# Another last instruction on GpSimd: a tensor_tensor on one column becomes an affine_select on a 128x128 mask

## The chip, the cores and the metric

The kernel runs on one core of one Trainium2 chip. The metric is the device time of one execution in microseconds (us), the median of three runs of the same program. One of the three is also recorded by the hardware profiler.

## What is computed

Three transformer layers in float32, on 256 tokens of width 1024:

```
x = first_block(x, ...)        # attention with causal mask and distance bias, then squared-ReLU MLP
return second_block(x, c, ...) # even_layer: gated convolution + RG-LRU, then SwiGLU
                               # odd_layer: stick-breaking attention, then SwiGLU
```

The first thing that happens to x is a norm and a projection, which is where this case plays:

```
def rms_norm(x, gain):
    y = xf * lax.rsqrt(jnp.mean(xf * xf, axis=-1, keepdims=True) + RMS_EPS)
u = rms_norm(h, norm_mix_pre[layer])
q, k, v = jnp.split(x @ w_qkv, 3, axis=-1)
```

The stick-breaking attention masks its scores strictly below the diagonal, `strict = k_pos < q_pos`. The two layers of the second block take shift, scale and gate vectors from `silu(c) @ ada_w + ada_b`.

## The kernel before

The program is written engine by engine: each engine has one in-order instruction stream, and semaphores tie them together. There is no scheduler. The 256 tokens are two tiles of 128 (t = 0, 1). All weights (about 205 MB) stream from HBM through four buffers `w_raw`. ScalarE (ACT) rounds each part to `w_hi` (line 747), VectorE (DVE) computes the remainder `w_lo` (line 1178), and TensorE (PE) multiplies hi by hi, hi by lo and lo by hi.

The **start**. GpSimd (POOL) makes the constants. It writes `ones` (line 665, semaphore `consts` becomes 1), clears `ident` (line 667), turns it into the identity with an affine_select (line 668), clears `rg_w` (line 670, `consts` becomes 2), fills `neg_dist` with iota (lines 673 and 675), builds `sb_mask` (lines 677 and 678), masks `neg_dist` (line 682), and then three times clears 2048 columns of `mod` and loads a bias row into them (lines 631 and 632). PE waits for `consts` 1, runs two warm-up matmuls (line 2236) and spreads the gain row over the partitions (line 2241). Then it waits for `consts` 2, since everything that follows begins with transposes of the normed x by the identity: `norm_T` (line 1940), four transposes for each half of a tile. ACT copies them out of PSUM to `aT` (line 811), and PE starts on the products of the first projection (line 2064). ACT's own order there is: squares and rstd of tile 0 (lines 769, 853 and 854), w_hi of weight parts 0 and 1 (line 747), aT (line 811), squares of tile 1.

The **middle**. POOL adds up the partitions of the partial sums of `ada_w` with partition_all_reduce (line 661), in groups spread over the program, and between the groups it does small tensor_scalar and tensor_tensor operations for the norms (lines 643 and 652 to 655) and some memsets.

The **end of POOL's program**. `partition_sums` for `GATE_F` (line 661, two instructions) and then one tensor_tensor on `var[:, 0:1]` (line 721), whose result nobody reads. POOL has nothing after that.

The built program has an extra POOL instruction at several places, which the source does not write: it is shown as `ISA` without operands and as MODIFY_POOL_CONFIG in the trace. One stands before the first affine_select (line 668), one before each group of partition_all_reduce (line 661), and one before the first tensor_scalar or tensor_tensor that follows such a group (lines 643, 652 and 721). In this text it is called the reload. The two kinds are told apart by what follows: into set A (iota, tensor_scalar, tensor_tensor) and into set B (partition_all_reduce). Memset and DMA have none anywhere.

Of the kernel before, what the change touches and what calls it, by code (L numbers as in the profile page):

```python
# [28 lines left out]
ALU = mybir.AluOpType  # L29
# [3 lines left out]
P = 128  # L33
# [10 lines left out]
NEG = -1e30  # L44
# [70 lines left out]
def block_program(nc, a, out):  # L115
    ctx = ExitStack()
    with ctx:
        def sb(name, shape, dt=F32):
            return ctx.enter_context(nc.sbuf_tensor(name, shape, dt))
# [28 lines left out]
        sb_mask = sb("sb_mask", [P, P])  # L148
# [5 lines left out]
        half_sums = sb("half_sums", [P, 4])  # L154
        var = sb("var", [P, 2])
# [260 lines left out]
        def parts_to(u, i=None, per=0):  # L416

            return plus(2 * u, i, 2 * per)
# [199 lines left out]
        def _(pool):  # L618
# [38 lines left out]
            def partition_sums(src, dst, done, count, step):  # L657

                for n in range(src.shape[-1] // CH):
                    pool.wait_ge(done, count + step * n)  # L660
                    pool.partition_all_reduce(dst[:, n * CH:(n + 1) * CH], src[:, n * CH:(n + 1) * CH], P,  # L661
                                              bass.bass_isa.ReduceOp.add).then_inc(pool_sum, 1)
# [6 lines left out]
                                       base=0, pattern=[[-1, P]], channel_multiplier=1))  # L669
# [9 lines left out]
                               pattern=[[-1, P]], channel_multiplier=1).then_inc(consts, 1)  # L679
            for lo, n, q0 in ((0, P, 0), (P, TOK, P)):  # L680
                part = neg_dist[:, lo:lo + n]
                pool.affine_select(out=part, in_=part, compare_op=ALU.is_ge, fill=NEG, base=q0,
                                   pattern=[[-1, n]], channel_multiplier=1).then_inc(consts, 1)
# [34 lines left out]
            rstd_halves()  # L718
            pool.wait_ge(xn_done, 24)
            partition_sums(GATE_F, GATE_F, w_used, parts_to(U_SG1 + 8), 6)  # L720
            pool.tensor_tensor(var[:, 0:1], half_sums[:, 1:2], half_sums[:, 0:1], ALU.add)


        @block.scalar
# [1794 lines left out]
```

## Time and profile before

| | us |
|---|---|
| median of 3 runs | 879.93 |
| lowest and highest | 879.71 and 880.51 |
| the profiled execution, its own time | 880.51 |
| its span in the trace | 878.7 |
| PE busy in the span | 869.1 (99%) |
| POOL busy in the span | 112.7 (13%) |

The span counts from the start of the recording to the last instruction's end; 1.81 us of the profiled execution's own time lie outside it. Busy time of PE includes waits inside its pipeline; what can be read safely is when its groups start. In a row of the timeline the two first numbers are start and duration in us, and the bracket behind it is the idle time of that engine before it with what ended it; "issue" means that it waited for nothing that the profile shows. PEld is the weight load of TensorE, and an engine's name with a q behind it is its sequencer.

### The profile page before, as it was taken

What the parts mean: (1) busy time and instruction counts of PE and PEld (TensorE: products, weight loads), DVE (VectorE), ACT (ScalarE), POOL (GpSimd) and SP (SyncE); (2) the same over time, 40 slices, a digit from 0 to 9 for tenths busy, and PEclk for the clock granted to TensorE, in tenths of its full rate; (3) what the DMA queues carried; (4) which work ended last, traced back from release to release, by engine and by line L of the source; (5) the groups of instructions that cost most, each with busy time, mean ns of one, the idle gap of its engine ahead of it and who ended that gap; (6) DMA issues with size and microseconds to landing.
All of it is one profiled execution on the core that took longest, in us unless ns stands there. A gap on an engine that the chain in (4) does not pass through costs nothing.

```text
span 878.7 us, 13239 instructions
## 1 busy us (share of the span) xinstructions
PE 869.1 (99%) x4806; PEld 739.7 (84%) x4806; DVE 714.6 (81%) x737; ACT 490.6 (56%) x663; POOL 112.7 (13%) x79
## 2 busy tenths in 40 slices
PE   8999999999999999999999999999999999999998
PEld 5998878888888799979888888878777888888887
DVE  6698987999898987898989899787897866655656
ACT  6545665565556657755555455555775365545542
POOL 5000100032110103026010411012000101100000
PEclk9999999999999999999999999999999999999999
DMA  7979567899889484547998798546434386666662
GB/s 243 346 248 355 173 211 296 319 366 358 322 324 339 159 287 146 176 160 216 386 329 309 269 353 302 180 137 216 135 113 142 96 245 190 190 192 190 191 192 72
DMA packets 117238, 208.07 MB, mean 237 GB/s; under 512 B 7252, under 2 KB 81340, under 8 KB 112072
## 3 DMA queue, kind: packets, MB, share of 16 engines
q1 hardware_dynamic: 116710, 205.31, 68.7%
q10 hardware_dynamic: 290, 2.10, 0.7%
q8 instruction: 28, 0.46, 0.2%
q14 instruction: 18, 0.15, 0.1%
q0 software_dynamic: 192, 0.05, 0.0%
HBM read 206.39 MB, written 1.05 MB: 236 GB/s over the span
## 4 chain that ended last, share of the span: by engine, by line
PE 93%; DVE 3%; DMA 2%; ACT 1%; issue 1%; POOL 0%; SPq 0%; DVEq 0%; POOLq 0%
PE ub L1968 11%; PE tp L1968 11%; PE acc L1826 7%; PE acc L1827 7%; PE acc L1829 7%; PE ub L1970 5%; PE tp L1970 5%; PE acc L1789 5%; PE acc L1790 5%; PE acc L1791 5%; PE acc L1954 3%; PE acc L1956 3%; PE acc L1955 3%; PE tp L2031 2%; PE acc L2064 1%; PE acc L1982 1%
## 5 line engine op out<-in xcount | busy, mean ns | idle before, releaser
L1178 DVE TENSOR_TENSOR w_lo<-w_raw,w_hi 128x1024 fp32r<-128x1024 f32 x271 | 343.3, 1283 | 78.1 <-ACT w_hi L747 77.6
L747 ACT ACTIVATE w_hi<-w_raw 128x1024 fp32r<-128x1024 f32 x271 | 283.9, 1056 | 202.7 <-PE acc L1829 41.5
L1968 PE MATMUL tp<-aT,w_hi 128*128 128x512 f32 x432 | 135.9, 396 | 0.0
L1968 PE MATMUL ub<-aT,w_hi 128*128 128x512 f32 x432 | 135.4, 395 | 0.0
L1826 PE MATMUL acc<-w_hi,hT_hi 128*128 128x512 f32 x266 | 103.9, 390 | 0.7 <-DVE w_lo L1178 0.7
L1827 PE MATMUL acc<-w_lo,hT_hi 128*128 128x512 f32 x266 | 103.6, 389 | 0.0
L1829 PE MATMUL acc<-w_hi,hT_lo 128*128 128x512 f32 x262 | 101.9, 389 | 0.0
L1970 PEld LDWEIGHTS tp<-aT,w_lo 128*128 128x128 f32 x432 | 81.2, 188 | 19.2
L1970 PEld LDWEIGHTS ub<-aT,w_lo 128*128 128x128 f32 x432 | 81.1, 188 | 18.9
L661 POOL PARTITION_ALL_REDUCE mod<-mod x14 | 57.9, 4133 | 259.1 <-PE tp L1970 117.6
L1970 PE MATMUL tp<-aT,w_lo 128*128 128x256 f32 x432 | 84.9, 278 | 0.0
L1970 PE MATMUL ub<-aT,w_lo 128*128 128x256 f32 x432 | 84.9, 278 | 0.0
L1968 PEld LDWEIGHTS ub<-aT,w_hi 128*128 128x128 f32 x432 | 67.6, 189 | 2.0
L1968 PEld LDWEIGHTS tp<-aT,w_hi 128*128 128x128 f32 x432 | 65.8, 189 | 0.0
L1826 PEld LDWEIGHTS acc<-w_hi,hT_hi 128*128 128x128 f32 x266 | 49.9, 188 | 10.7 <-DVE w_lo L1178 0.8
L1357 DVE SCALAR_TENSOR_TENSOR mod<-ada_raw,silu_c,mod 128x2048 f32<-128x2048 f32 x24 | 58.3, 2430 | 0.3 <-DVE mod L1357 0.2
L1829 PEld LDWEIGHTS acc<-w_hi,hT_lo 128*128 128x128 f32 x262 | 49.2, 188 | 10.4
L1827 PEld LDWEIGHTS acc<-w_lo,hT_hi 128*128 128x128 f32 x266 | 49.9, 188 | 9.3
L1954 PE MATMUL acc<-aT,w_hi 128*128 128x256 f32 x192 | 55.3, 288 | 0.0
L1956 PE MATMUL acc<-aT,w_lo 128*128 128x256 f32 x192 | 54.3, 283 | 0.0
L1955 PE MATMUL acc<-aT,w_hi 128*128 128x256 f32 x192 | 54.3, 283 | 0.0
L1789 PE MATMUL acc<-w_hi,aT 128*128 128x512 f32 x128 | 51.9, 406 | 0.0
(327 smaller groups left out, 1427.7 us busy)
## 6 DMA issues: line engine op xcount, KB each, us to landing
ada_raw<-in_l_ada_w SPq DMA_DIRECT2D x24, 1024.0 KB, 6.2
w_raw<-in_l_ffn_w_gate SPq DMA_DIRECT2D x44, 512.0 KB, 4.6
w_raw<-in_l_ffn_w_up SPq DMA_DIRECT2D x44, 512.0 KB, 4.5
w_raw<-in_l_ffn_w_down SPq DMA_DIRECT2D x44, 512.0 KB, 4.0
w_raw<-in_w_up SPq DMA_DIRECT2D x32, 512.0 KB, 4.5
w_raw<-in_w_down SPq DMA_DIRECT2D x32, 512.0 KB, 5.7
scratch<-in_l_ada_w SPq DMA_DIRECT2D x14, 1024.0 KB, 7.7
w_raw<-in_attn_w_qkv SPq DMA_DIRECT2D x24, 512.0 KB, 6.1
```

What stands on the lines that cost most here:

```text
L747: act.activation(rounded_part(v), w_raw[:, v % SLOTS, :], ACT.Copy).then_inc(hi_done, 1)
L1178: dve.tensor_tensor(rest_part(v), w_raw[:, v % SLOTS, :], rounded_part(v).bitcast(F32), ALU.subtract).then_inc(lo_done, 1)
L1357: dve.scalar_tensor_tensor(part, ada_slot[slot] if src is None else src, silu_c[:, bass.ds(col, 1)], part, ALU.mult, ALU.add).then_inc(ada ...
L1789: pe.matmul(outp, op_hi[:, k + n, q], wh[:, c], start=start and n == 0, stop=False)
L1826: pe.matmul(outp, operand[0][:, k, q], wh[:, c], start=start, stop=False)
L1827: last = pe.matmul(outp, operand[0][:, k, q], wl[:, c], start=False, stop=False)
L1829: last = pe.matmul(outp, operand[1][:, k, q], wh[:, c], start=False, stop=stop)
L1954: pe.matmul(outp, wh, aT_hi[:, b, :], start=b == 0, stop=False)
L1955: pe.matmul(outp, wh, aT_lo[:, b, :], start=False, stop=False)
L1956: last = pe.matmul(outp, wl, aT_hi[:, b, :], start=False, stop=b == KB - 1)
L1968: pe.matmul(banks[f], rounded_part(v)[:, c[f]], aT[:, :, b, :], start=b == 0, stop=False)
L1970: last = pe.matmul(banks[f][:, 0:TOK], rest_part(v)[:, c[f]], aT_hi[:, b, :], start=False, stop=b == KB - 1)
```

## The change

The last instruction of POOL's stream is another one. Before, it adds two columns of `half_sums` into column 0 of `var`, 128x1. Now it repeats, in place, the affine_select of line 678 on `sb_mask`, 128x128. Neither has a semaphore on it.

```diff
             pool.wait_ge(xn_done, 24)
             partition_sums(GATE_F, GATE_F, w_used, parts_to(U_SG1 + 8), 6)
-            pool.tensor_tensor(var[:, 0:1], half_sums[:, 1:2], half_sums[:, 0:1], ALU.add)
+            pool.affine_select(out=sb_mask[:, :], in_=sb_mask[:, :], compare_op=ALU.is_ge, fill=NEG, base=-1,
+                               pattern=[[-1, P]], channel_multiplier=1)
```

What it makes of POOL's stream is more than the diff says. This is the end of that stream, before (-) and now (+); a row names line, operation, output and input:

```order
 L661 ISA
 L661 ISA mod<-mod 128x512 x2
-L721 ISA
-L721 TENSOR_TENSOR var<-half_sums 128x1
+L721 AFFINE_SELECT sb_mask<-sb_mask 128x128
 L117 UNCONDITIONAL_BRANCH
```

Two rows have become one: the reload ahead of line 721 is gone too, so the reload ahead of line 661 (into set B) is now the last one of the program. An affine_select gets no reload behind partition_all_reduce.

The beginning of the same stream is the same in both but for the numbers of lines:

```order
L667 MEMSET ident 128x128 [waits pool_chain]
L668 ISA [waits pool_chain]
L668 AFFINE_SELECT ident<-ident 128x128
L670 MEMSET rg_w 128x1024 [waits pool_chain]
L673 IOTA neg_dist 128x128
L675 IOTA neg_dist 128x256 [waits pool_chain]
```

Here the reload (into set A) stands between the clearing of `ident` and the affine_select that makes the identity. Nothing moved here, nor on any other engine.

## Rows read from the trace of the kernel before

**Rows 1.** The page: the chain that ended last, by engine, and the busy times
```profile
PE 869.1 (99%) x4806; PEld 739.7 (84%) x4806; DVE 714.6 (81%) x737; ACT 490.6 (56%) x663; POOL 112.7 (13%) x79
PE 93%; DVE 3%; DMA 2%; ACT 1%; issue 1%; POOL 0%; SPq 0%; DVEq 0%; POOLq 0%
```

**Rows 2.** The chain in order of time, first 14 us: start, us, what
```profile
1.66 6.48 DMA w_raw<-in_attn_w_qkv
8.17 1.06 ACT w_hi L747
9.22 0.49 ACT aT L811
9.76 3.06 PE acc L2064 x12
```

**Rows 3.** Timeline of POOL, the end of its stream
```profile
753.86 3.23 POOL L661 PARTITION_ALL_REDUCE mod<-mod  x1 [13.22 <-PE acc L1829]
765.14 0.18 POOL L721 TENSOR_TENSOR var<-half_sums 128x1 f32<-128x1 f32 x1 [8.05 <-issue]
```

**Rows 4.** The reloads at lines 721, 668 and 661 (390 to 400 us): ns min/median/max, start
```profile
L721 POOLq MODIFY_POOL_CONFIG  x2: 87/88/88, 757.0 to 757.1; - x2
...
L668 POOLq MODIFY_POOL_CONFIG  x2: 11/11/11, 1.7 to 1.7; - x2
...
L661 POOLq MODIFY_POOL_CONFIG  x2: 37/37/37, 396.8 to 396.8; - x2
```

**Rows 5.** Timeline of POOL, the start
```profile
1.06 0.20 POOL L667 MEMSET ident<- 128x128 f32 x1
1.75 0.29 POOL L668 TENSOR_SCALAR_AFFINE_SELECT ident<-ident 128x128 f32<-128x128 f32 x1 [0.49 <-POOL ident L667]
2.11 0.95 POOL L670 MEMSET rg_w<- 128x1024 f32 x1
3.01 0.47 POOL L673 IOTA neg_dist<- 128x128 f32 x1
...
4.67 0.64 POOL L682 TENSOR_SCALAR_AFFINE_SELECT neg_dist<-neg_dist 128x128 f32<-128x128 f32 x2
...
12.95 0.48 POOL L632 DMA_DIRECT2D mod<-in_l_ada_b  x1 [0.29 <-POOL mod L631]
```

**Rows 6.** Timeline of POOL, the reload of line 661 that nothing covers
```profile
395.79 0.71 POOL L632 DMA_DIRECT2D mod<-in_l_ada_b  x1 [0.29 <-POOL mod L631]
403.30 3.25 POOL L661 PARTITION_ALL_REDUCE gate_ffn<-mod  x1 [6.80 <-issue]
```

**Rows 7.** Timeline of PE, PEld, ACT and SP's queue, the start
```profile
1.02 3.44 PE L2236 MATMUL ub<-ones 128*128 128x512 f32 x4 [1.02 <-POOL ones L665]
4.30 1.88 PE L2241 MATMUL acc<-gain,ones 128*128 128x512 f32 x4
6.97 0.42 PEld L1940 LDWEIGHTS tp<-ident,xn 128*128 128x128 f32 x4 [1.62 <-issue]
12.43 1.02 PEld L1940 LDWEIGHTS ub<-ident,xn 128*128 128x128 f32 x8
...
8.17 1.06 ACT L747 ACTIVATE w_hi<-w_raw 128x1024 fp32r<-128x1024 f32 x1 [1.02 <-DMA w_raw<-in_attn_w_qkv]
9.13 0.58 ACT L811 ACTIVATE aT<-tp 128x512 fp32r<-128x512 f32 x1
13.29 1.09 ACT L811 ACTIVATE aT<-ub 128x512 fp32r<-128x512 f32 x2 [0.55 <-PE ub L1940]
...
19.88 0.27 SPq L506 DMA_DIRECT2D scratch<-in_c  x1
```

**Rows 8.** Busy us and counts by stretch; last three: granted clock, DMA share, GB/s
```profile
1.30:9.30 8.00, 6.10 (x16) 2.62 (x16) 4.72 (x6) 5.12 (x8) 6.89 (x11) 1.00 0.93 323
396.50:403.30 6.80, 6.80 (x55) 6.63 (x54) 5.22 (x5) 3.26 (x3) 0.00 (x1) 1.00 0.97 302
757.00:765.00 8.00, 8.00 (x48) 6.98 (x48) 4.54 (x5) 3.82 (x6) 0.09 (x1) 1.00 0.60 178
```

**Rows 9.** First readers of neg_dist and mod, readers of sb_mask: ns, first and last start
```profile
L1448 DVE SCALAR_TENSOR_TENSOR scratch<-neg_dist,ub x8: 542/547/555, 47.2 to 90.6; 128x384 f32<-128x384 f32 x8
...
L1369 DVE SCALAR_TENSOR_TENSOR mod<-ada_raw,silu_c,mod x3: 1275/1278/1284, 37.6 to 53.2; 128x1024 f32<-128x1024 f32 x3
...
L1728 DVE TENSOR_TENSOR ub<-ub,sb_mask x8: 672/694/700, 628.1 to 662.1; 128x512 f32<-128x512 f32 x8
```

**Rows 10.** Weight loads and matmuls of lines 2236 and 2241: ns min/median/max
```profile
L2236 PEld LDWEIGHTS ub<-ones x4: 286/335/337, 1.0 to 2.9; 128*128 128x128 f32 x4
L2236 PE MATMUL ub<-ones x4: 724/1061/1220, 1.0 to 3.7; 128*128 128x512 f32 x4
...
L2241 PEld LDWEIGHTS acc<-gain,ones x4: 190/190/320, 3.7 to 5.2; 128*128 128x128 f32 x4
L2241 PE MATMUL acc<-gain,ones x4: 592/592/593, 4.3 to 5.6; 128*128 128x512 f32 x4
```

## The prediction

> **What bounds the kernel now.** I read the chain that ended last first. By engine it is PE 93%, POOL 0% [rows 1]: GpSimd is nowhere on it, and it is busy for 13% of the span. So neither the old nor the new last instruction can cost anything by its own duration. It stands at 757 to 765 us of 878.7 [rows 3], and nothing follows it on POOL. The edit looks like one that does nothing. What made me read on is the second view, the change in POOL's stream: a reload has disappeared with the old instruction. So I looked at what a reload costs, and for the place where one would be paid.
>
> **What a reload costs.** Before line 721 the trace shows POOL idle for 8.05 us, from the end of the last partition_all_reduce (753.86 + 3.23 = 757.09) to 765.14, and the idle time is put down to nothing that the profile shows [rows 3]. The reload's own record sits at the front of that gap, at 757.0 to 757.1, and lasts 88 ns [rows 4]. So the record is short and the cost lies behind it: 8.05 us from B to A. The opposite way, A to B, has one uncovered case too: its record is at 396.8, and the partition_all_reduce starts at 403.30, so 6.50 us [rows 4, 6]. All other reloads have their cost hidden in long waits for PE or ACT.
>
> **What the start shows.** The reload into set A at line 668 has its record at 1.7, and the affine_select starts at 1.75 [rows 4, 5]. It cost nothing, and the iota of line 673, which belongs to set A alone, starts 3.01 without a gap as well [rows 5]. So set A was there already when this execution began. The stream of before ends in set A, since its last reload is the one at line 721. The stream of after ends in set B. If what one execution leaves is what the next one finds, the start of after has a true reload, B to A, in the place where before has an empty one. That is my mechanism: the last instruction of one execution prepares the first stage of the next.
>
> **The change part by part.**
>
> Removed at the end: one reload (8.05 us) and one tensor_tensor of 0.18 us; added: one affine_select, 0.29 us by its twin at line 668 [rows 3, 5]. All of this runs on POOL behind its last duty, over 110 us ahead of the end, and no engine waits for it: 0. The mask it rewrites is last read at 662.1 + 0.7 us [rows 9] and is built anew by each execution. Cover would be gone only if POOL's tail were longer than those 110 us. Freed DMA or memory traffic at 757 us: 0, since PE is the bound there.
>
> Added at the start: the reload. I go step by step.
> 1. The record stands at 1.70. With 8.05 us the affine_select starts at 9.75 instead of 1.75: 8.00 later.
> 2. From the affine_select to `consts` 2 are the 0.36 us to line 670 and its 0.95 us: before, 3.06; after, 11.06. PE reacts to such a signal in about 0.06 us (ones is ready 0.96, PE starts 1.02), so the weight load of the first transpose starts at 11.12. Before, it started at 6.97 [rows 5, 7]. It didn't wait for POOL then, but for the normed x: 3.9 us of the delay are hidden there, and 4.15 are left.
> 3. From transposes to ACT's copy: where all eight come in a row, 12.43 to 13.29, it is 0.86 us [rows 7]. So ACT copies at 11.98. Before, at 9.13: it wasn't the transposes that held it, but ACT's own order, behind the w_hi of 8.17 whose weights landed at 8.14 [rows 2, 7]. That hides another 1.3 us, leaving 11.98 - 9.13 = 2.85.
> 4. From ACT's copy PE follows after 9.76 - 9.13 = 0.63 us [rows 2, 7]: the first product starts at 12.61, 2.85 later than now.
>
> So of a reload of L us the first 5.2 are hidden, and the rest, L - 5.2, is on the path. Behind this point PE runs without a gap: twelve products in 3.06 us, and so on [rows 2]. ACT, DVE and the weight stream follow PE (their buffers come free by its work), so I take the shift as rigid to the end. What else waits for POOL's start has room: `neg_dist` is first read at 47.2, POOL would have it at 4.67 + 0.64 + 8.00 = 13.3; the bias rows in `mod` are first read at 37.6 and their last load issued by 12.95 + 0.48 + 8.00 = 21.4 [rows 5, 9]. SP waits for `consts` 2 behind its load of 19.88, long after 11.06 [rows 7].
>
> **The size of L.** The ends are 6.50 us [rows 4, 6], which gives 1.3, and something above 8.05. At the start the DMA engines are busier, share 0.93 against 0.60 at 757 us [rows 8]; if the reload's time went with that share, L would be 8.05 x 0.93 / 0.60 = 12.5 and the shift 7.3. But the 6.50 us case ran at share 0.97, which speaks against such a slope. I take 8.05, the only row that goes the same way, B to A: **2.85 us**.
>
> [...]
>
> The sum on the profiled execution: 880.51 + 2.85 = 883.36. That execution lies 0.58 above the median, so I give 879.93 + 2.85 = **882.8 us**.
>
> **The rivals.**
>
> *The state isn't kept* (the side of no change). Set A may be there at every start because whatever prepares an execution puts it there, or the timed run may follow something else than itself. The trace shows one start, and it can't tell "left by the last run" from "put there anew". For it: the source asks for a reload at the start in any case. Against: the reload of line 668 is in the program and was found empty, and nothing in the 1.7 us before it loads anything. Then nothing changes: 879.9. The price is all or nothing, and it decides at L's visibility: below L = 5.2 + 1.76 = 7.0 us the delay would be under 0.2% as well.
>
> [...]
>
> *A longer reload*, 10 to 12.5 us under the start's traffic: 884.7 to 887.2.
>
> *A shorter one, or a shift that is partly made up*: at 6.50 us the time is 881.2. In the same way, a stage that waits for DMA could give some of the shift back, since the stream starts on time.
>
> *Faster*: only by freed traffic near 757 us or noise; no row supports it.
>
> **How the numbers follow.** About 0.2% (1.8 us) is what a measurement of this kernel can tell from no change. Chances: forecast 0.35 (881.8 to 883.8), with the clock's fall 0.28 (883.8 to 885.4), longer reload 0.08, short or made up 0.10 (880.5 to 881.7), state not kept 0.17 (879.5 to 880.3), faster 0.02. Slower is 0.35 + 0.28 + 0.08 = 0.71, same 0.10 + 0.17 = 0.27. To leave out no more than 2 in 10 the range must take in the case of no change, so it goes from 879.6 to 885.6; it leaves out most of the longer reload. For the cases in which the state is kept the range is 881.0 to 885.6.
>
> **What the profile would show.** At the start: POOL idle for about 8.5 us before the affine_select of line 668 (0.49 now), the first transposes at 11.1, the copy of line 811 at 12.0, the first product at 12.6 us, and from there all rows of before, shifted by one amount; no reload at line 721. Step 1 is wrong if that gap stays at 0.5. Step 3 is wrong if the products start later than 0.9 + 0.6 us behind the transposes. [...] A shift that shrinks between 13 us and the end would show a wait for weights that absorbed it, most likely before 160 us. The prediction fails as a whole if the affine_select starts at 1.75 as now.

## The result and the profile after

| | before | after |
|---|---|---|
| median, us | 879.88 (6 runs) | 887.56 (6 runs) |
| lowest and highest | 879.71 and 880.51 | 886.22 and 888.43 |
| the profiled execution, its own time | 880.51 | 888.13 |
| its span | 878.7 | 886.3 |

The ratio is 1.0085, with a 95% interval of 1.0072 to 1.0098: the change costs 7.7 us (6.3 to 8.6 by the interval). The forecast was 882.8, in a range from 879.6 to 885.6, so the result lies above it. The sign and the mechanism came out as forecast; the size is 7.7 us where 2.85 was given.

The page of after differs from [rows 1] in its chain: POOL and "issue" have a share of 1% more each, and DMA has fallen from 2% to 0%.

```profile
PE 871.8 (98%) x4806; PEld 741.8 (84%) x4806; DVE 714.5 (81%) x737; ACT 490.3 (55%) x663; POOL 110.9 (13%) x79
...
PE 92%; DVE 3%; issue 2%; ACT 1%; POOL 1%; DMA 0%; DVEq 0%; POOLq 0%; SPq 0%; ACTq 0%
```

The chain of after in order of time (start, us, what), to be held against [rows 2]. The change is one line longer, so lines behind 721 are counted one higher.

```profile
1.52 12.09 issue
13.96 0.96 POOL rg_w L670
14.96 1.97 PE tp L1941 x8
16.93 4.12 PE acc L2065 x12
21.06 0.87 PE ub L1941 x8
```

Before, the chain began with a weight load from memory and ACT's w_hi. Now, behind POOL's first small memsets, come 12.09 us in which POOL waits for nothing that the profile shows, then `rg_w`'s memset, and only then TensorE's transposes. POOL's timeline, start and end of the stream, answers to [rows 5] and [rows 3]:

```profile
1.06 0.20 POOL L667 MEMSET ident<- 128x128 f32 x1
13.62 0.28 POOL L668 TENSOR_SCALAR_AFFINE_SELECT ident<-ident 128x128 f32<-128x128 f32 x1 [12.36 <-issue]
13.96 0.95 POOL L670 MEMSET rg_w<- 128x1024 f32 x1
...
761.47 3.23 POOL L661 PARTITION_ALL_REDUCE mod<-mod  x1 [13.22 <-PE acc L1830]
764.59 0.36 POOL L721 TENSOR_SCALAR_AFFINE_SELECT sb_mask<-sb_mask 128x128 f32<-128x128 f32 x1
```

At the end the gap of 8.05 us is gone: the new last instruction starts right behind the partition_all_reduce. At the start a gap has opened in its place, 12.36 us where 0.49 stood. The reload's own record is there in both kernels, 11 ns long [rows 4]:

```profile
L668 POOLq MODIFY_POOL_CONFIG  x2: 11/11/11, 1.5 to 1.5; - x2
```

So what moved is not an instruction but the 12.1 us behind a record (13.62 - 1.5). TensorE's timeline, the start (compare [rows 7]):

```profile
4.59 2.53 PE L2242 MATMUL acc<-gain,ones 128*128 128x512 f32 x4
14.96 1.97 PE L1941 MATMUL tp<-ident,xn 128*128 128x128 f32 x8 [7.84 <-POOL rg_w L670]
```

And busy us and counts by stretch of after (PE, PEld, DVE, ACT, POOL; then granted clock, DMA share, GB/s), to be held against [rows 8]:

```profile
6.00:8.00 2.00, 1.12 (x3) 0.19 (x1) 1.58 (x3) 1.05 (x1) 0.00 (x0) 1.00 1.04 392
8.00:10.00 2.00, 0.00 (x0) 0.00 (x0) 1.04 (x1) 1.06 (x1) 0.00 (x0) 0.83 1.02 374
10.00:12.00 2.00, 0.00 (x0) 0.00 (x0) 0.00 (x0) 0.00 (x0) 0.00 (x0) 0.50 1.03 365
...
16.00:18.00 2.00, 2.00 (x8) 1.57 (x7) 1.25 (x2) 1.85 (x4) 2.00 (x4) 0.50 0.00 0
18.00:20.00 2.00, 2.00 (x7) 1.53 (x7) 2.00 (x4) 1.72 (x4) 1.68 (x3) 0.61 0.15 15
20.00:22.00 2.00, 2.00 (x15) 1.75 (x13) 0.49 (x1) 0.47 (x1) 1.70 (x2) 1.00 0.75 251
```

From 10 to 12 us no compute engine does anything. TensorE, idle since about 7.1, has its clock at 0.50, and works at that level until about 19.5 us. Both things that the prediction kept apart, a longer reload and a fall of the clock, happened together.

**Where the 7.62 us of the two profiled executions come from.** The affine_select starts 13.62 - 1.75 = 11.87 us later. By steps 2 to 4 of the prediction 5.15 of a delay are hidden (8.00 in, 2.85 out), which leaves 6.72. The twelve first products end at 21.06 instead of 12.82, 8.24 later: the other 1.52 are work at the lower clock. Of these, 0.29 lie ahead of the first product: it starts at 16.77 instead of 9.76, 7.01 later, since from the transposes to it are 1.81 us instead of the 1.49 of the forecast. The other 1.23 lie in the products: from the start of the first to the end of the twelfth are 4.29 us (16.77 to 21.06) instead of 3.06. (The chain puts their beginning at 16.93, the end of the transposes.) Then something is given back. DVE's timeline of before and of after:

```profile
84.89 1.28 DVE L1369 SCALAR_TENSOR_TENSOR mod<-xn,silu_c,mod 128x1024 f32<-128x1024 f32 x1
86.09 0.68 DVE L1401 COPY scratch<-acc 128x512 f32<-128x512 f32 x1
```
```profile
91.96 1.28 DVE L1370 SCALAR_TENSOR_TENSOR mod<-xn,silu_c,mod 128x1024 f32<-128x1024 f32 x1
93.35 0.69 DVE L1402 COPY scratch<-acc 128x512 f32<-128x512 f32 x1
```

TensorE's timeline of the same place, of before and of after:

```profile
84.93 0.49 PE L2254 MATMUL tp<-ident,scratch 128*128 128x128 f32 x3
...
86.88 0.46 PE L2259 MATMUL acc<-ada_raw,scratch 128*128 128x128 f32 x2 [0.80 <-issue]
...
90.73 0.50 PE L1789 MATMUL acc<-w_hi,aT 128*128 128x512 f32 x1
```
```profile
93.15 0.49 PE L2255 MATMUL tp<-ident,scratch 128*128 128x128 f32 x3
...
94.14 0.46 PE L2260 MATMUL acc<-ada_raw,scratch 128*128 128x128 f32 x2
...
98.28 0.50 PE L1790 MATMUL acc<-w_hi,aT 128*128 128x512 f32 x1 [0.24 <-DVE aT L1187]
```

Before, DVE began the 1.28 us operation of line 1369 at 84.89, just ahead of the end of TensorE's projection, so the copy of v came 1.2 us late and TensorE stood still for 0.80 us. (The profile names no releaser there; the copy ends at 86.77 and TensorE starts at 86.88.) After, DVE's same operation is only 7.07 us later while TensorE is 8.22 later: the operation is over when the copy is wanted, and TensorE's wait is gone. The shift goes 8.22, 7.26, 7.55 at these three rows (0.24 is lost again to another wait for DVE), and it is 7.61 at POOL's last partition_all_reduce (761.47 against 753.86). So 6.72 + 1.52 - 0.62 = 7.62. The 0.62 is taken as what is left over; that it belongs to this place is read from the shifts, which are 8.22 ahead of it and 7.6 behind it up to the end (the spans differ by 7.6).

### The profile page after: what moved, and what is told of

It is laid out like the page before. It is cut to its first block, busy times and chain, and to the rows that moved or that the text cites. A ratio compares the mean times of both kernels' runs of the same rounds, so it can differ in the third digit from the quotient of the medians.

```text
span 886.3 us, 13238 instructions
## 1 busy us (share of the span) xinstructions
PE 871.8 (98%) x4806; PEld 741.8 (84%) x4806; DVE 714.5 (81%) x737; ACT 490.3 (55%) x663; POOL 110.9 (13%) x79
## 4 chain that ended last, share of the span: by engine, by line
PE 92%; DVE 3%; issue 2%; ACT 1%; POOL 1%; DMA 0%; DVEq 0%; POOLq 0%; SPq 0%; ACTq 0%
PE ub L1969 11%; PE tp L1969 11%; PE acc L1827 7%; PE acc L1828 7%; PE acc L1830 7%; PE ub L1971 5%; PE tp L1971 5%; PE acc L1790 5%; PE acc L1791 5%; PE acc L1792 5%; PE acc L1955 3%; PE acc L1957 3%; PE acc L1956 3%; PE tp L2032 2%; PE acc L2065 1%
```

## The experiments

Of each kernel the edit is shown against before or against after, as named, and longer edits are cut to their main lines. Each ratio is to runs of before that were made beside it, whose medians were 879.66 to 880.32 us. The lengths of a reload at the start count from its record at 1.5 us to the affine_select.

### What the last instruction leaves behind

**e1_no_last**, before without its last instruction:
```diff
-            pool.tensor_tensor(var[:, 0:1], half_sums[:, 1:2], half_sums[:, 0:1], ALU.add)
```


> The kernel before without its last GpSimd instruction; nothing takes its place, so the program ends in set B like the changed kernel. Residency theory (what one execution leaves is what the next one finds): the affine_select of line 668 starts near 13.6 us, 12.1 us behind its reload, and the time is about 887.5, as in the changed kernel. Rival (the affine_select on sb_mask itself does the harm, by its work or by what it writes): it is gone, so the time is that of before, 879.9, and line 668 starts at 1.75.

Measured: 888.39 us (4 runs), ratio 1.0097 [1.0080, 1.0114]. Removing a dead instruction costs as much as replacing it. POOL's timeline:
```profile
13.37 0.28 POOL L668 TENSOR_SCALAR_AFFINE_SELECT ident<-ident 128x128 f32<-128x128 f32 x1 [12.10 <-issue]
```

**e2_both**, after with the old instruction put back ahead of the new one:
```diff
+            pool.tensor_tensor(var[:, 0:1], half_sums[:, 1:2], half_sums[:, 0:1], ALU.add)
             pool.affine_select(out=sb_mask[:, :], in_=sb_mask[:, :], compare_op=ALU.is_ge, fill=NEG, base=-1,
```


> Both last instructions: the tensor_tensor of before with its reload into set A, and behind it the affine_select of the changed kernel. Residency theory: the program ends in set A, line 668 starts at 1.75, time 879.9. Rival (the affine_select itself): 887.5.

Measured: 880.01 us (10 runs), 0.9998 [0.9988, 1.0007]. The new last instruction is there and the loss is gone. So affine_select itself is free, and it leaves set A in place.
```profile
1.75 0.29 POOL L668 TENSOR_SCALAR_AFFINE_SELECT ident<-ident 128x128 f32<-128x128 f32 x1 [0.49 <-POOL ident L667]
```

**e3_set_b_last**, before with one partition_all_reduce more at its very end, which has its own reload into set B:
```diff
             pool.tensor_tensor(var[:, 0:1], half_sums[:, 1:2], half_sums[:, 0:1], ALU.add)
+            pool.partition_all_reduce(gate_ffn[:, 0:CH], gate_ffn[:, 0:CH], P, bass.bass_isa.ReduceOp.add)
```


> The kernel before, whole, with its old last instruction, and one more partition_all_reduce behind it on gate_ffn, which nobody reads any more. The program then ends in set B though every instruction of before is there. Residency theory: line 668 starts near 13.6, time about 887.5. Rival (the absence of the old last instruction or of its reload pair matters in another way): 879.9.

Measured: 887.81 us (4 runs), 1.0089 [1.0072, 1.0105], the affine_select at 13.05 us. Here nothing of before was taken away: the two reloads at the end are both present, with a third, into set B, behind them. Together the three say it from every side: ending in A costs nothing at the start, ending in B costs 7.7 to 8.5 us, whatever instruction ends it. This rules out the rival that the state isn't kept.

### Whether the lateness of the identity is all of it

**e6_memsets** delays the affine_select of before by plain work, with no reload in the place:
```diff
+            for _ in range(6):
+                chained(pool.memset(mod[:, 0:UNIT], 0.0))
```


> The kernel before, ending in set A, with six memsets of 128x2048 on GpSimd between the clearing of ident and its affine_select: the same lateness of the signal consts 2 (about 6 x 2.1 = 12 us) without any reload. If all of the loss is the lateness of that signal with what hangs on it (transposes, the TensorE clock), the time is 887 to 888, the first product starts near 17 us, and the granted clock falls to 0.50 in the gap. Rival (a true reload also slows the loads of x and weights or something else in the start): clearly below 887.

Measured: 887.91 us (4 runs), 1.0089 [1.0073, 1.0106]. POOL's timeline:
```profile
1.32 11.44 POOL L669 MEMSET mod<- 128x2048 f32 x6
13.25 0.29 POOL L670 TENSOR_SCALAR_AFFINE_SELECT ident<-ident 128x128 f32<-128x128 f32 x1 [0.49 <-POOL mod L669]
```
Nearly the same lateness made otherwise (11.50 us against 11.87) gives the same time (887.91 against 887.56). The reload does harm by nothing but the time at which `ident` is ready; it takes nothing from the weight loads that could be measured here.

**e12_memsets4** is the same with four memsets, 7.77 us of delay, which is nearly the 8.00 of the prediction:
```diff
+            for _ in range(4):
+                chained(pool.memset(mod[:, 0:UNIT], 0.0))
```


> The kernel before with four memsets of 128x2048 on GpSimd between the clearing of ident and its affine_select, a delay of about 8 us, which is what the prediction took for the reload. By the prediction's own steps (the first 5.2 us are hidden) the first product comes 2.8 us late and the time is 882.6, or 884.2 if the clock falls in the gap of 4.9 us. Rival (the hidden part is wrong, the whole delay counts): 887.8.

Measured: 884.26 us (5 runs, 883.56 to 884.79), 1.0052 [1.0038, 1.0066]. This is the case of the prediction's L = 8.05. TensorE's timeline and two stretches of it:
```profile
10.88 1.41 PE L1942 MATMUL tp<-ident,xn 128*128 128x128 f32 x8 [4.28 <-POOL rg_w L672]
12.22 2.08 PE L2066 MATMUL acc<-w_hi,aT 128*128 128x512 f32 x4
```
```profile
10.00:12.00 2.00, 1.12 (x8) 1.00 (x8) 0.00 (x0) 0.43 (x1) 1.72 (x5) 0.88 1.01 360
12.00:14.00 2.00, 2.00 (x6) 1.49 (x5) 1.80 (x3) 1.94 (x6) 2.00 (x4) 0.50 0.18 60
```
The first product starts 12.22 - 9.76 = 2.46 us later; the steps give 7.77 - 5.15 = 2.62. So the 5.15 hidden microseconds are confirmed to within 0.2. And behind an idle time of only 4.28 us the clock falls from 1.00 over 0.88 to 0.50: it still reads 1.00 up to 11 us, falls while the transposes run, and stands at 0.50 where the products run. They take 1.2 us more than before (next transposes at 16.33 instead of 12.66, 3.67 later, of which 2.46 is the first product's shift). The median lies in the range that the prediction gave to the clock's fall, 883.8 to 885.4; the five runs spread over 1.2 us.

**e7_pe_busy** is after, with 8 matmuls of ones (16 in the trace) in the gap of TensorE:
```diff
+            warm_up(8)
             pe.wait_ge(consts, 2)
```


> The changed kernel with eight more warm-up matmuls on PE ahead of its wait for consts 2 (about 6.8 us of work in the gap of 7.8 us). Clock theory: the granted clock no longer falls to 0.50 between 8 and 19 us, the first twelve products take 3.06 us rather than 4.12 and the transposes half their 1.97, so the time falls by 1 to 1.8 us to about 886. Rival (the clock costs nothing, all is the late signal): 887.5 as in the changed kernel.

Measured: 886.14 us (5 runs, 886.00 to 887.08), 1.0070 [1.0056, 1.0084]. TensorE's timeline and one stretch:
```profile
14.89 1.09 PE L1941 MATMUL tp<-ident,xn 128*128 128x128 f32 x8 [0.80 <-POOL rg_w L670]
16.24 1.20 PE L2065 MATMUL acc<-w_hi,aT 128*128 128x512 f32 x4 [0.25 <-ACT aT L812]
```
```profile
16.00:18.00 2.00, 1.76 (x8) 1.45 (x9) 1.78 (x3) 1.94 (x6) 2.00 (x4) 1.00 0.00 0
```
The transposes start 0.07 us earlier than in after and last 1.09 instead of 1.97 us. The median is 1.4 us below after's and the span 1.6 (884.7 against 886.3), but the intervals of the two ratios, 1.0070 and 1.0085, overlap, so the times alone don't settle it. The trace does: from the first transposes to the next ones (19.12 here, 20.89 in after) are 4.23 us instead of 5.93, 1.7 less; the sum above says 1.52. So the price of the lower clock is about 1.5 us here: from 16 to 18 us it reads 0.50 in after and 1.00 in this run.

**e8_ident_signal** is after, with the signal of `ident` given ahead of `rg_w`'s memset (SP and DVE count one more):
```diff
-            chained(pool.affine_select(out=ident[:, :], in_=ident[:, :], compare_op=ALU.not_equal, fill=1.0,
-                                       base=0, pattern=[[-1, P]], channel_multiplier=1))
+            pool.affine_select(out=ident[:, :], in_=ident[:, :], compare_op=ALU.not_equal, fill=1.0,
+                               base=0, pattern=[[-1, P]], channel_multiplier=1).then_inc(consts, 1)
```


> The changed kernel with the signal consts 2 given by the affine_select that makes ident, ahead of the 0.95 us memset of rg_w instead of behind it; SP and DVE wait for one count more. If PE's start stands and falls with that signal, everything comes 0.95 us earlier: about 886.6. If something else is as late (x, weights, ACT), nothing changes: 887.5.

Measured: 886.60 us (5 runs, 886.07 to 888.62), 1.0085 [1.0071, 1.0099]. In the trace the products start 1.22 us sooner than in after (15.55 against 16.77), 0.20 of it by a shorter reload, and the span is 1.5 us less. The ratio is the same as after's. The trace shows the step, the times don't resolve it.

### What makes the reload 12.1 us long at the start

In after, SP issues six loads of 512 KB in the first 4 us, two of x and four of weights, and a seventh at 9.07 us, while the reload runs. These kernels hold the six back. Only the length of the reload is read from them; their own times mean little, since the held loads are late. **e4_quiet** issues none until `ident` is there, **e5_x_only** the two of x:
```diff
+            sp.wait_ge(consts, 2)
             load_x(0)
             proj_half(U_QKV1, qkv1, 0, 0)
```


> The changed kernel, but SP starts its first load only when consts is 2, so no weights or x are moved while the reload runs. To be read is the time from the reload's record to the affine_select of line 668. Traffic theory (the reload took 12.1 us at the start because it shares the way to memory with the first loads): about 6 to 8 us. Rival (12.1 us is what the first reload of an execution costs, whatever runs beside it): 12. The total is of no interest here, since all loads start late.


```diff
             load_x(0)
-            proj_half(U_QKV1, qkv1, 0, 0)
             load_x(1)
+            sp.wait_ge(consts, 2)
+            proj_half(U_QKV1, qkv1, 0, 0)
```


> As the kernel with quiet loads, but the two loads of x (1 MB) go at once and only the weights wait for consts 2. Traffic theory: the reload's time lies between, about 8 to 10 us, since the traffic ends after some 4 us. Rival (a fixed 12.1 us): 12.

The others let each load wait until the one k places before it has landed; `first` lists the six loads with their semaphores (its definition is cut here):
```diff
+            for n, (load, _) in enumerate(first):
+                if n >= k:
+                    sp.wait_ge(first[n - k][1], 16)
+                load()
```
With k = 1, 2, 3 and 4:

> As the kernel with two on the way, but with one. Queue theory: 7 to 8 us, hardly above the 6.9 us without any traffic. Rival: half speed as long as the loads last, which is longer now: 12 us or more.

> The changed kernel with at most two of SP's first six loads on the way at a time; before, six are issued within 3 us. The same 3 MB move while the reload runs. Queue theory (a reload goes at half its speed while many transfers stand in the queues, and at full speed in the middle of the program, where two or three are on the way at 292 GB/s): 7 to 9 us from the record to the affine_select. Rival (at the start any traffic slows it, the number on the way doesn't matter): half speed until the 3 MB are through, 12 us.

> As the kernel with four on the way, with three. Queue theory: about 9.5 to 10.5 us. Rival (rate alone): at nearly 300 GB/s about 11 to 12.

> The changed kernel with at most four of SP's first six loads on the way. The memory rate should be that of the changed kernel (about 300 GB/s), so rate and number on the way come apart. Queue theory: the reload takes longer than with two on the way (8.9 us) and less than with all six (12.1), about 10 to 11. Rival (it goes by the rate alone): about 12.

Measured, one run with its profile of each (share and rate over the reload; for after the time is the median):

| kernel | loads on the way | reload, us | DMA share | GB/s | time, us |
|---|---|---|---|---|---|
| e4_quiet | 0 | 6.9 | 0.00 | 1 | 891.26 |
| e11_one_ahead | 1 | 7.3 | 0.44 | 146 | 885.72 |
| e5_x_only | 2, then none | 8.6 | 0.34 | 122 | 890.87 |
| e10_two_ahead | 2 | 8.9 | 0.81 | 254 | 884.78 |
| e14_three_ahead | 3 | 10.35 | 0.94 | 320 | 887.20 |
| e13_four_ahead | 4 | 11.85 | 0.90 | 310 | 888.69 |
| after | all six | 12.1 | 0.89 | 304 | 887.56 |

The stretches of e4_quiet, e14_three_ahead, e13_four_ahead and after:
```profile
1.50:8.40 6.90, 5.61 (x8) 1.88 (x7) 1.18 (x3) 1.10 (x1) 0.00 (x0) 1.00 0.00 1
```
```profile
1.50:11.85 10.35, 5.59 (x8) 1.90 (x7) 3.82 (x6) 4.76 (x7) 0.00 (x0) 0.87 0.94 320
```
```profile
1.50:13.35 11.85, 4.65 (x8) 1.55 (x7) 3.73 (x6) 4.76 (x7) 0.00 (x0) 0.89 0.90 310
```
```profile
1.50:13.60 12.10, 5.62 (x8) 1.89 (x7) 3.81 (x6) 4.86 (x7) 0.00 (x0) 0.82 0.89 304
```
The reload needs 6.9 us with nothing on the way, and the loads of this kernel make it 12.1. The same six loads gave 11.85 in e1_no_last and 11.55 in e3_set_b_last, so one profile is good to about half a microsecond, and four ahead and six can't be told apart. What sets the addition is not the mean rate: three ahead moves more bytes a second than four ahead or all six and has a shorter reload, and the two loads of x alone cost nearly as much as two ahead at twice the rate. It follows the number of loads on the way, some 1.5 us for each from the second to the fourth. All loads are of 512 KB, so their number and the bytes that wait were not told apart. In e5_x_only nothing moves from 5 us on (0 GB/s), and yet the reload ends at 10.10 where it ended at 8.41 without loads: so at least there, what lengthened it happened in its first 3.5 us. The expectation for four ahead, 10 to 11 us, was too low.

**e9_probes** asks the same in the middle of the program: before, with a one-column iota behind four groups of partition_all_reduce, which forces an uncovered reload into set A:
```diff
+                pool.iota(probe[:, n:n + 1], pattern=[[1, 1]], base=0, channel_multiplier=0,
+                          allow_small_or_imprecise_dtypes=True)
```


> The kernel before with an iota on one column, waiting for nothing, behind four groups of partition_all_reduce: the gap before each is the bare time of a reload into set A, at four levels of traffic in the middle of the program. Traffic theory: the times grow with the DMA share of their stretch, from about 8 us at a share of 0.6 to 12 us near 1. Rival (the start is special): all four are 8 to 9 us whatever the traffic. Program time as before, 879.9, since the gaps lie in waits.

Measured: 879.24 us, one run, as before. POOL's timeline and two of the stretches:
```profile
265.57 0.14 POOL L663 IOTA probe<- 128x1 f32 x1 [8.22 <-issue]
349.67 0.14 POOL L663 IOTA probe<- 128x1 f32 x1 [7.00 <-issue]
539.71 0.14 POOL L663 IOTA probe<- 128x1 f32 x1 [7.09 <-issue]
621.80 0.14 POOL L663 IOTA probe<- 128x1 f32 x1 [7.47 <-issue]
```
```profile
257.34:265.57 8.23, 8.23 (x40) 6.88 (x39) 6.20 (x6) 5.69 (x6) 0.01 (x2) 1.00 0.84 307
```
```profile
532.62:539.71 7.09, 7.09 (x41) 6.12 (x40) 6.78 (x6) 3.29 (x4) 0.00 (x1) 1.00 0.78 292
```
In the middle, B to A takes 7.0 to 8.2 us, and at nearly one rate (307 and 292 GB/s) once 8.22 and once 7.09; the other two, at 134 and 146 GB/s, took 7.00 and 7.47. So neither the growth up to 12 us nor the rival's 8 to 9 us came out. The 8.05 of [rows 3] is one of this family. None of them reaches 12: the start is another situation. Why a reload takes longer with more loads on the way, and where in its course, was not found.

### Mending it, and the idle time that took some back

**e15_mended** is after, still ending in set B, with three edits at once: two loads ahead (k = 2), `ident`'s own signal, and `warm_up(4)` ahead of TensorE's wait.

> The changed kernel, still ending in set B, with three things at once: two loads on the way, four more warm-up matmuls on PE in the gap, and the signal consts 2 ahead of the clearing of rg_w. If the parts add up: transposes start near 10.75 us at full rate, the first product near 12.2, and the time is 880 + 12.2 - 9.8 - 0.7 = 881.7 to 882.5. If one of them only hides behind another, 884 or more.

Measured: 882.31 us (11 runs, 881.59 to 884.55), 1.0025 [1.0015, 1.0034]. TensorE's timeline and its clock:
```profile
10.63 1.04 PE L1946 MATMUL tp<-ident,xn 128*128 128x128 f32 x8
11.92 1.20 PE L2070 MATMUL acc<-w_hi,aT 128*128 128x512 f32 x4 [0.25 <-ACT aT L817]
```
```profile
12.00:14.00 2.00, 2.00 (x9) 1.65 (x10) 2.00 (x3) 1.94 (x6) 1.85 (x4) 1.00 0.76 229
```
It wins back 887.56 - 882.31 = 5.25 of the 7.68 us, but one dead instruction at the end, as before has it, does better than all three together. What each of the three contributes was not measured.

**e16_copy_first** takes DVE's copy of v ahead of the operation of line 1369 in before, to remove TensorE's wait of 0.80 us:
```diff
-... G8 L12 A4 S5 G9
-    U11 E5 A5 ...
+... G8 L12 A4 S5
+    U11 E5 G9 A5 ...
```


> The kernel before with one exchange on DVE at 85 us: the copy of v (line 1401) ahead of a scalar_tensor_tensor of 1.28 us on mod (line 1369). In the trace of before PE idles 0.8 us there until that copy is done, in the changed kernel it doesn't. If this idle time is what gives 0.7 us of the delay back, this kernel is faster than before by up to 0.7 us, about 879.2; rival (PE waits there for something else): 879.9.

Measured: 880.67 us (11 runs, 879.63 to 882.58), 1.0004 [0.9995, 1.0013]: no gain. DVE's timeline shows the two in their new order:
```profile
87.50 0.69 DVE L1401 COPY scratch<-acc 128x512 f32<-128x512 f32 x1 [1.04 <-PE acc L1791]
88.11 1.27 DVE L1369 SCALAR_TENSOR_TENSOR mod<-xn,silu_c,mod 128x1024 f32<-128x1024 f32 x1
```
TensorE's wait of 0.80 us is gone there, but another for DVE has come in its place:
```profile
92.73 0.50 PE L1789 MATMUL acc<-w_hi,aT 128*128 128x512 f32 x1 [0.53 <-DVE aT L1186]
```
From the transposes of line 2254 to this product are 5.42 us (87.31 to 92.73), where before has 5.80 and after 5.13. So only 0.4 us are left of the gain in the trace, and the times show none. That the 0.6 us given back in after come from this place rests on the two traces, where the shift falls at these rows; no run has tested it by itself. None of the kernels is measurably faster than before.

## Why the prediction came out as it did

- **The mechanism, and where to look**: right. The chain by engine showed POOL at 0%, and the two instructions cost nothing by themselves. What counted was the reload that vanished from the order, and e1 to e3 show that the set which the last reload leaves is what the next execution finds: the affine_select of line 668 starts at 13.37, 1.75 and 13.05 us. The rival that the state isn't kept (0.17) is out.
- **The end of the stream costs nothing**: right. The new instruction takes 0.36 us (0.29 was given), directly behind the reduction, and no one waits.
- **Steps 2 to 4, 5.2 us hidden**: right. In e12_memsets4 a delay of 7.77 gives 2.46 (2.62 by the steps). That run has no reload and ends as before does, so it tests these steps alone. In after 11.87 leaves 6.72, and with about 0.3 for transposes at the lower clock the first product is due 7.0 us late; it was 7.01.
- **"The size of L"**: this term failed. It was taken at 8.05 us and measured 12.1. The upper end, 12.5, was in the text, but was left with a chance of 0.08, because the 6.50 us case of [rows 6] ran at a share of 0.97 and spoke against a slope with DMA share. That argument was sound against the share, and e13_four_ahead, e14_three_ahead and e9_probes bear it out; but it doesn't follow that the start is like the middle. No row showed a reload with six fresh loads issued in one burst at the same moment, and an unknown with no row of its own kind deserved an open upper end. The error is 11.87 - 8.00 = 3.87 us, four fifths of the whole miss of 4.8.
- **The clock's fall**: this second term was put at nothing in the sum of the forecast. It had a chance of 0.28 as a case beside it, at 883.8 to 885.4, 1.0 to 2.6 us above the 882.8. No row of before shows the clock fall or what that costs, so those figures were the author's estimate. What could be read was that the first four matmuls have a median of 1061 ns and the next four one of 592 [rows 10]. The runs showed 1.52 us in after and 1.2 in e12_memsets4, with the clock at 0.50. So the case was right in kind and near in size, and e12_memsets4 shows that it comes already at L = 8.05, behind a gap of 4.28 us. It belonged in the forecast itself: with L as assumed and the clock's fall, e12_memsets4 has 884.26.
- **How the numbers follow**: the rivals were priced one at a time. In after the longer reload came with a gap of 7.84 us and the clock at 0.50. The 887.2 of the rival for 12.5 us lacked it; with the 1.52 of after it would have been 888.7. The upper end of 885.6 held neither the longer reload nor the two together. The chances by sign (0.71 slower) served.
- **The rigid shift**: nearly right; 8.24 at 21 us became 7.6 at the end, by a wait of TensorE for DVE at 86 us that vanished.
- **The lengths of a reload that were seen**: the shortest reload into set A of any run here took 6.9 us, with nothing on the DMA engines, and the shortest into set B 6.50 [rows 4, 6]; the longest took 12.1.

## What to carry to other kernels

Look at the set of the last reload of a GpSimd program and the set that its start needs first: a dead instruction at the end that reloads the first stage's set under cover was worth 7.7 us here, at a reload of 12.1 and with the clock's fall counted in, and three other edits together recovered only 5.25 of them. Price a reload by a row taken under the same burst of loads, and where there is none, leave the upper end open. When a delay opens a gap in front of TensorE, add the lower clock to that same case, not as a rival to it: behind gaps of 4.28 and 7.84 us it cost 1.2 and 1.5 us here.

## What the runs showed of the hardware that was not expected

- The set of one execution's last reload was there at the start of the next, as the prediction supposed: the affine_select of line 668 starts at 13.37, 13.05 and 13.62 us where that reload was into set B (e1, e3, after), and at 1.75 where it was into A (before, e2).
- A reload into set A takes 6.9 us with the DMA engines idle, 7.0 to 8.2 in the middle of the program, and 11.55 to 12.1 with six loads of 512 KB issued close behind each other; at the start it follows the number of loads on the way (or their bytes), not the rate.
- TensorE's clock fell to 0.50 around a gap of 3.9 us without work (e11_one_ahead, 0.50 from 10 to 11 us) and of 4.3 us (e12_memsets4), as in one of 7.8 us (after); it stayed at 1.00 over the gap of 1.5 us in before; with matmuls of no use in the gap it stayed at 1.00 (e7_pe_busy, e15_mended).
